# Token-tile-wise transposes and waits at each normalised input of a two-block transformer kernel

## The reference

```
def rms_norm(x, g):
    xf = x.astype(jnp.float32)
    y = xf * lax.rsqrt(jnp.mean(xf * xf, axis=-1, keepdims=True) + EPS)
    return (y * g.astype(jnp.float32)).astype(x.dtype)
...
        u = rms_norm(h, ffn_norm_g[i])
        h = h + swiglu(u, ffn_w_gate[i], ffn_w_up[i], ffn_w_down[i])
        gate = jax.nn.sigmoid(rms_norm(h, ple_norm_g[i]) @ ple_w_gate[i])
        h = h + gate * (p[i] @ ple_w_proj[i])
```

## Time and profile before

| | |
|---|---|
| median of 3 runs | 1090.81 us (1090.73 to 1091.69) |
| the profiled execution | 1090.82 us |
| its span | 1088.8 us |
| TensorE busy | 1061.1 us, 97% |
| VectorE, ScalarE, GpSimd busy | 65%, 50%, 2% |
| chain that ended last | TensorE 88%, VectorE 7%, ScalarE 3% |
| mean granted clock of TensorE | 0.997 |

### The profile page before, as it was taken

The page is one execution under the profiler, slowest core; times in us unless marked ns, Lnnn a source line. Parts: engine busy times, 40 slices in busy tenths (PEclk is TensorE's granted clock), DMA queues, the critical chain, the costliest instruction groups (busy, mean ns, idle before and its releaser), DMA issues.

```text
span 1088.8 us, 13626 instructions
## 1 busy us (share of the span) xinstructions
PE 1061.1 (97%) x5484; PEld 899.6 (83%) x5484; DVE 706.8 (65%) x996; ACT 540.7 (50%) x698; POOL 22.6 (2%) x34
## 2 busy tenths in 40 slices
PE   8999899999999999999999999999999999999997
PEld 7998778888887778778888887878888888999886
DVE  5999875544548787776454545767554475777654
ACT  5853654444445666755444434565444553434533
POOL 1000310000000000000000000000000000000000
PEclk9999999999999999999999999999999999999999
DMA  8631365555553453256554555366545455455530
GB/s 322 193 100 39 106 223 197 190 193 193 193 175 144 151 188 117 78 199 246 193 193 174 179 191 191 122 216 232 191 177 194 157 191 193 157 192 193 194 116 39
DMA packets 27829, 188.68 MB, mean 173 GB/s; under 512 B 3016, under 2 KB 4168, under 8 KB 5880
## 3 DMA queue, kind: packets, MB, share of 16 engines
q1 hardware_dynamic: 24912, 179.32, 45.8%
q0 software_dynamic: 1392, 6.21, 1.7%
q10 hardware_dynamic: 1464, 2.30, 1.2%
HBM read 185.19 MB, written 2.62 MB: 173 GB/s over the span
## 4 chain that ended last, share of the span: by engine, by line
PE 88%; DVE 7%; ACT 3%; issue 1%; POOL 0%; ACTq 0%; POOLq 0%; DVEq 0%
PE bank L254 27%; PE bank L256 26%; PE bank L255 26%; PE bank L444 4%; DVE w_lo L1212 3%; PE bank L296 2%; ACT w_hi L764 1%; PE bank L361 1%; PE bank L417 1%; DVE x_lo L1268 1%; DVE arena L1258 1%; ACT x_hi L782 0%; PE bank L502 0%; ACT arena L953 0%; PE bank L458 0%
## 5 line engine op out<-in xcount | busy, mean ns | idle before, releaser
L1212 DVE TENSOR_TENSOR w_lo<-raw,w_hi 128x2048 fp32r<-128x2048 f32 x169 | 389.5, 2309 | 217.3 <-ACT w_hi L764 216.6
L764 ACT ACTIVATE w_hi<-raw 128x2048 fp32r<-128x2048 f32 x169 | 322.4, 1910 | 163.2 <-PE bank L256 156.9
L254 PE MATMUL bank<-w_hi,x_hi 128*128 128x512 f32 x800 | 318.2, 398 | 7.3 <-DVE x_lo L1268 4.8
L256 PE MATMUL bank<-w_hi,x_lo 128*128 128x512 f32 x800 | 313.1, 391 | 0.0
L255 PE MATMUL bank<-w_lo,x_hi 128*128 128x512 f32 x800 | 312.2, 390 | 0.0
L254 PEld LDWEIGHTS bank<-w_hi,x_hi 128*128 128x128 f32 x800 | 150.5, 188 | 42.8 <-issue 6.9
L256 PEld LDWEIGHTS bank<-w_hi,x_lo 128*128 128x128 f32 x800 | 150.6, 188 | 32.4
L255 PEld LDWEIGHTS bank<-w_lo,x_hi 128*128 128x128 f32 x800 | 150.7, 188 | 29.4
L254 PE MATMUL bank<-w_hi,z_hi 128*128 128x512 f32 (+1 forms) x368 | 143.0, 389 | 3.3 <-DVE h L1339 1.5
L256 PE MATMUL bank<-w_hi,z_lo 128*128 128x512 f32 (+1 forms) x368 | 141.7, 385 | 0.0
L255 PE MATMUL bank<-w_lo,z_hi 128*128 128x512 f32 (+1 forms) x368 | 141.6, 385 | 0.0
(11 more groups left out here) (209 smaller groups left out, 791.6 us busy)
## 6 DMA issues: line engine op xcount, KB each, us to landing
raw<-in_ws SPq DMA_DIRECT2D x169, 1024.0 KB, 4.8
arena<-in_rows POOLq DMA_DIRECT2D x2, 1024.0 KB, 5.6
toep<-bias_row ACTq DMA_DIRECT2D x1, 1536.0 KB
h<-in_x_tok SPq DMA_DIRECT2D x2, 512.0 KB, 4.6
arena<-in_rows POOLq DMA_DIRECT2D x2, 512.0 KB, 7.2
arena<-toep POOLq DMA_DIRECT2D x1, 1024.0 KB, 6.8
out<-arena SPq DMA_DIRECT2D x2, 512.0 KB, 2.9
arena<-in_pool_m POOLq DMA_DIRECT2D x1, 768.0 KB, 4.4
```

Of the source, the lines that this page charges most:

```text
L254: pe.matmul(dst, s_hi, m_hi, start=first, stop=False)
L256: return pe.matmul(dst, s_lo, m_hi, start=False, stop=last)
L764: act.activation(w_hi[:, g % SPLIT, :], raw[:, g % RAW, :], ACT.Copy).then_inc(hi_done, 1)
L1212: dve.tensor_tensor(w_lo[:, g % SPLIT, :], raw[:, g % RAW, :], w_hi[:, g % SPLIT, :].bitcast(F32), ALU.subtract).then_inc(lo_done, 1)
```

## The change

It does five things.
- The two transposes of a half are issued apart (`h_job`): half 0 has tile 0 after a = 0 and tile 1 after (1, 0) of the last chunk, or before each of the two last groups of the FFN's down projection; half 1 has tile 0 after (0, 0) and tile 1 after (0, 1) of the first chunk. `ready(a, t)` waits for one tile.
- The gain is multiplied in place in the PSUM bank; `x_hi` and `x_lo` are read from the bank, and `stage` is gone. A bank is now free for the next transpose after the low part (`x_split`), no longer after the gain.
- The factor is made on GpSimd by an addition, a scaling and a power, and VectorE's `h_factor` is gone.
- The low part of two of the 169 weight pieces (`POOL_LO`, the second piece of either PLE) is subtracted on GpSimd. `lo_ready` waits for the right semaphore, SyncE's loads too.
- GpSimd waits for `r_done` before two loads into the second block's tables.

```
+POOL_LO = [G["ffn0"] + 34, G["ffn1"] + 34]
...
+        def lo_ready(eng, g):
+            if g in POOL_LO:
+                eng.wait_ge(S("lo_pool"), POOL_LO.index(g) + 1)
+            else:
+                eng.wait_ge(lo_done, g + 1 - len([p for p in POOL_LO if p < g]))
...
                 for a in range(2):
-                    if ready:
-                        ready(a)
-                    pe.wait_ge(lo_done, g0 + a + 1)
+                    lo_ready(pe, g0 + a)
                     s = (g0 + a) % SPLIT
                     for t in range(TT):
                         b = t
+                        if ready:
+                            ready(a, t)
...
-                end(("tr",) + key, b, ins)
                 if gain:
                     count["gain"] += 1
                     jobs[key] = (S("x_split"), count["gain"])
-                else:
+                end(("tr",) + key, b, ins, release=jobs.get(key))
...
-                return {(0, 0): [lambda: h_jobs(m, n)]}
+                return {(0, 0): [h_job(m, n, 0)], (0, 1): [h_job(m, n, 1)]}
...
+                                if i == GU - 1 and n == 1:
+                                    h_job(m + 1, 0, t)()
...
-                token_chunk(("ple", layer, 1), g0 + 2, x_hi, x_lo, between=lambda: h_jobs(m + 1, 0))
+                token_chunk(("ple", layer, 1), g0 + 2, x_hi, x_lo, between=h_job(m + 1, 0, 0),
+                            hooks={(1, 0): [h_job(m + 1, 0, 1)]})
...
+            def factor(m):
+                c = 4 * (m % 2)
+                pool.wait_ge(S("h_ss"), 4 * m + 4)
+                link(pool.tensor_tensor(st[:, 8:10], st[:, c:c + 2], st[:, c + 2:c + 4], ALU.add))
+                link(pool.tensor_scalar(st2[:, 60:62], st[:, 8:10], 1.0 / D, EPS, ALU.mult, ALU.add))
+                pool.tensor_tensor(st2[:, 2 * m:2 * m + 2], st2[:, 60:62], st2[:, 56:58], ALU.pow).then_inc(S("r_done"), 1)
+
+            def low(g):
+                pool.wait_ge(hi_done, g + 1)
+                pool.tensor_tensor(w_lo[:, g % SPLIT, :], raw[:, g % RAW, :], w_hi[:, g % SPLIT, :].bitcast(F32),
+                                   ALU.subtract).then_inc(S("lo_pool"), 1)
...
-                dve.tensor_tensor(stage[:, s, :].rearrange("p (k c) -> p k c", k=4),
-                                  bank[:, :].rearrange("p (k c) -> p k c", k=4),
-                                  gain.unsqueeze(2).to_broadcast([P, 4, P]), ALU.mult).then_inc(free, 1)
+                bank, _ = take(dve, ("tr",) + key)
+                v = bank[:, :].rearrange("p (k c) -> p k c", k=4)
+                dve.tensor_tensor(v, v, gain.unsqueeze(2).to_broadcast([P, 4, P]), ALU.mult).then_inc(S("gained"), 1)
...
                 for n in range(2):
                     for t in range(TT):
                         add_h(("ffn", layer, n, t), n, t)
-                    if n == 0:
-                        h_split(m + 1, 0, gname)
-                h_split_factor(m + 1, gname)
+                    h_split(m + 1, n, gname)
```

More of the change, by code:

```diff
@@ L300, in transpose_job @@
                     jobs[key] = (S("x_split"), count["gain"])
-                else:
+                end(("tr",) + key, b, ins, release=jobs.get(key))
+                if not gain:
                     jobs[key] = released[b]
@@ L305, in h_release, with h_job, ready @@
                 return lambda t: (S("h_done"), 4 * m + 2 * n + t + 1)
-            def h_jobs(m, n):
-                for t in range(TT):
-                    transpose_job((m, n, t), h[:, t, n * 512:(n + 1) * 512], (S("h_done"), 4 * m + 2 * n + t + 1), True)
+            def h_job(m, n, t):
+                return lambda: transpose_job((m, n, t), h[:, t, n * 512:(n + 1) * 512],
+                                             (S("h_done"), 4 * m + 2 * n + t + 1), True)
             def ready_from(m):
-                def ready(a):
-                    wait_job((m, a, 0), (m, a, 1))
+                def ready(a, t):
+                    wait_job((m, a, t))
                 return ready
@@ L398, in ffn @@
                 down(5)
-                h_jobs(m + 1, 0)
             def ple(layer, m):
@@ L484, in _, with z_ready @@
             keep_warm(32, 7)
-            def z_ready(a):
+            def z_ready(a, t):
                 pe.wait_ge(S("v_split"), 2 * a + 2)
             token_chunk(("pw2", 0), G["pw2"], z_hi, z_lo, ready=z_ready, release=h_release(0, 0))
-            token_chunk(("pw2", 1), G["pw2"] + 2, z_hi, z_lo, between=lambda: h_jobs(0, 0), release=h_release(0, 1))
+            token_chunk(("pw2", 1), G["pw2"] + 2, z_hi, z_lo, between=h_job(0, 0, 0),
+                        hooks={(1, 0): [h_job(0, 0, 1)]}, release=h_release(0, 1))
             ffn(0, 0)
@@ L569, in _, with o_ready @@
             projection(1, G["proj1"], (4, 5, 6, 7), between=lambda: o_jobs(0))
-            def o_ready(a):
-                wait_job(("o", a, 0), ("o", a, 1))
+            def o_ready(a, t):
+                wait_job(("o", a, t))
             token_chunk(("wo", 0), G["wo"], z_hi, z_lo, ready=o_ready, hooks={(0, 0): [lambda: o_jobs(1)]}, release=h_release(3, 0))
-            token_chunk(("wo", 1), G["wo"] + 2, z_hi, z_lo, between=lambda: h_jobs(3, 0), release=h_release(3, 1))
+            token_chunk(("wo", 1), G["wo"] + 2, z_hi, z_lo, between=h_job(3, 0, 0),
+                        hooks={(1, 0): [h_job(3, 0, 1)]}, release=h_release(3, 1))
             ffn(1, 3)
@@ L609, in job_ready, with ready @@
             def job_ready(name):
-                def ready(a):
-                    wait_job((name, a, 0), (name, a, 1))
+                def ready(a, t):
+                    wait_job((name, a, t))
                 return ready
@@ L640, in _ @@
             g = G["poolw"]
-            pe.wait_ge(lo_done, g + 1)
+            lo_ready(pe, g)
             for w in range(4):
@@ L721, in _ @@
                     pool.tensor_tensor(h[:, t, c], h[:, t, c], row_b2[:, c], ALU.add).then_inc(S("h_biased"), 1)
-            pool.wait_ge(S("h_done"), 4)
+            def factor(m):
[8 more added lines that the diff above has]
+                                   ALU.subtract).then_inc(S("lo_pool"), 1)
+            factor(0)
             pool.wait_ge(S("toep_out"), 16)
@@ L729, in _ @@
                 .then_inc(S("ld_toep"), 16)
+            low(POOL_LO[0])
+            factor(1)
+            factor(2)
+            factor(3)
+            pool.wait_ge(S("r_done"), 4)
             pool.wait_ge(S("h_done"), 16)
@@ L736, in _ @@
             pool.memset(sgu_t[HD:P, :, 0:HD], 0.0).then_inc(S("sgu_masked"), 1)
+            pool.wait_ge(S("sgu_masked"), 1)
+            low(POOL_LO[1])
+            factor(4)
+            factor(5)
             pool.wait_ge(S("h_done"), 24)
@@ L776, in table @@
                 act.activation(st[:, c:c + 1], ident[:, 0:1], func)
+            gains = [0]
             def split_hi(key, dst, k0, w):
-                freed(act, ("tr",) + key)
-                src = stage[:, job_no[key] % 2, :].rearrange("p (k c) -> p k c", k=4)
-                act.activation(dst[:, k0:k0 + 4, w], src, ACT.Copy).then_inc(S("t_hi"), 1)
+                bank, _ = take(act, ("tr",) + key)
+                gains[0] += 1
+                act.wait_ge(S("gained"), gains[0])
+                act.activation(dst[:, k0:k0 + 4, w], bank[:, :].rearrange("p (k c) -> p k c", k=4), ACT.Copy).then_inc(S("t_hi"), 1)
             def h_split(m, n):
@@ L1210, in feed @@
                     g = fed[0]
+                    fed[0] += 1
+                    if g in POOL_LO:
+                        continue
                     dve.wait_ge(hi_done, g + 1)
@@ L1248, in _ @@
             hi_count = [0]
-            stage_read = [0, 0]
-            split_count = [0]
             def gain_block(key, gain):
-                bank, free = take(dve, ("tr",) + key)
-                s = job_no[key] % 2
-                if stage_read[s]:
-                    dve.wait_ge(S("x_split"), stage_read[s])
-                dve.tensor_tensor(stage[:, s, :].rearrange("p (k c) -> p k c", k=4),
-                                  bank[:, :].rearrange("p (k c) -> p k c", k=4),
-                                  gain.unsqueeze(2).to_broadcast([P, 4, P]), ALU.mult).then_inc(free, 1)
+                bank, _ = take(dve, ("tr",) + key)
+                v = bank[:, :].rearrange("p (k c) -> p k c", k=4)
+                dve.tensor_tensor(v, v, gain.unsqueeze(2).to_broadcast([P, 4, P]), ALU.mult).then_inc(S("gained"), 1)
+            gains_read = [0]
             def split_lo(key, hi, lo, k0, w):
-                s = job_no[key] % 2
+                bank, _ = take(dve, ("tr",) + key)
                 hi_count[0] += 1
-                split_count[0] += 1
-                stage_read[s] = split_count[0]
+                gains_read[0] += 1
+                dve.wait_ge(S("gained"), gains_read[0])
                 dve.wait_ge(S("t_hi"), hi_count[0])
-                dve.tensor_tensor(lo[:, k0:k0 + 4, w], stage[:, s, :].rearrange("p (k c) -> p k c", k=4),
```

(1 more changed line is left out.)

26 lines of the change are left out of this document (7 added, 19 removed).

## The result

The changed kernel takes 1108.91 us (median, 1107.67 to 1109.53) against 1090.77 for the kernel before on the same chip: ratio 1.0163, 95% interval 1.0145 to 1.018, slower by 18.1 us. The profiled execution took 1108.43.

What follows compares the result with a forecast made beforehand. The prediction took TensorE as the bound, busy 1061.1 of 1088.8 us. Its terms summed to 11.7 us, with two clock falls 14.8, added to the median of 1090.81: forecast 1105.5 us, range 1098 to 1111.

Steps and rivals of the forecast that it cites:

- (a): Half 1 at all six transitions: a new TensorE stall of 1.6 us ahead of (1, 0), six times.
- (b): First and fourth transition: additions queued behind VectorE's late low parts and weight piece delay TensorE; cost 3.7 us each.
- (c): Second transition, into the first PLE: earlier start, mostly paid back by the new stall; gain 0.9 us.
- (d): Fifth transition: same gain as at the second, plus a clock fall avoided; gain 2.1 us.
- (e): Third and sixth transition: tile 1's late x_hi, at the third also holding ScalarE's queue; cost 3.4 and 2.9 us.
- (f): Kernel start: third and fourth transposes wait for low parts, so pw1 starts at 20.1 us; cost 1.7 us.
- (g): Attention's output projection: it waits for one tile, so its wait shrinks by one low part; gain 0.7 us.
- (h): Clock: TensorE's new stands bring two falls of the granted clock, costing 3.1 us together.
- (i): Parts counted at nothing: factor move, bank reads and writes, split transposes, and GpSimd's piece, taken as 11.0 us but hidden.
- rival 3: At the second and fifth transition GpSimd's weight piece binds: at 16.5 us it gives 1113 us; chance 0.04.
- Rival 1: More clock falls behind the long stands: five instead of two, giving 1110 us; chance 0.09.
- Rival 2: TensorE's waits go and nothing takes their place, so the kernel is faster: 1083.3 us; chance 0.07.

Runs made afterwards that it cites:

- e1_inter: Changed kernel with VectorE doing gain, low part, gain, low part by tile, in place of both gains then both low parts; 1100.09 us, ratio 1.0103.
- e4_token: Kernel before with only the transposes and waits by tile; no scaling in place, roots and all low parts on VectorE; 1112.18 us, ratio 1.0204.
- e11_first_fourth: Changed kernel with VectorE's queue at the first and fourth transition alone reordered: gain, low part, addition by tile, weight's low part last; 1101.12 us.
- e2_pair: Changed kernel with the two tiles' transposes issued together again, all else kept; 1089.44 us, ratio 0.9987.
- e6_queues: Changed kernel, still tile by tile, with VectorE's and ScalarE's queues put in the same tile order and the start's four jobs in four banks; 1087.34 us.
- e5_pair_banks: e2_pair with the start's third and fourth transpose jobs in banks 5 and 6; 1085.02 us, ratio 0.9951.
- e9_mixed: e5_pair_banks with tile-wise transposes only inside the last down projections, VectorE there taking gain, low, gain, low; 1081.47 us, ratio 0.9923.
- e10_half1_pair: e6_queues with the second half's transposes in pairs again and gain, gain, low, low for that half; 1077.79 us, ratio 0.9886.

## Why the prediction was right, and where its sizes were off

The sign and the mechanism held; the forecast of 1105.5 was 3.4 us short, inside its range. No error hid another: the sizes that were off lie mostly on the same side.

- **(a)** Predicted 1.6 us six times; the trace has 1.47 or 1.48 six times, and e1_inter removed all six. What that is worth is another thing: half of it came back at the chunks behind, and 4.3 us were won.
- **(b)** Predicted 3.7 at the first and fourth transition; 5.32 and 5.46 with a fall of about 1.6 each, 3.7 and 3.9 without. e4_token, with no fall there, has 3.76 and 3.68.
- **(c), (d)** Predicted -0.9 and -2.1; -0.92 and -2.15.
- **(e)** Predicted 3.4 and 2.9; 3.49, and 4.35 of which a fall is 1.5.
- **(f)** Mis-sized: predicted 1.7, found 2.4 in the table and 2.7 from the first block of busy work on. The prediction let the second block of busy work run for 2.40 us as before; after the stand of 3.83 it ran at a granted clock of 0.50 for the most part and took 3.64. The six kernels with this stand show 3.31 to 3.66, those without it 2.40.
- **(g)** Mis-sized: predicted 0.7, found 0.38. The projection starts 0.66 earlier, gives 0.65 back at the transposes of the second half, which wait for VectorE's work on the attention's output, then gains 0.3, and ends 0.38 ahead.
- **(h)** Mis-sized, the largest miss: two falls predicted, three came, 1.5 us more. The cause was right (e11_first_fourth). The count was a guess from one fall in two stands: stands of 2.4 us were followed by a fall at T1, T4 and T6 and not at T3, and two of the four executions, at 1109.4 and 1109.53 us with a mean granted clock of 0.990 instead of 0.992, had by estimate one more. The Trainium skill ("TensorE: Matmul & The Clock Gate", Part 1) says of a kernel's start that the number of slow matmuls differs from run to run. Behind stands in the middle of a kernel these runs agree: e1_inter took 1099.95 to 1105.99 us with the same instructions, at mean granted clocks of 0.995 and 0.990.
- **(i)** The 11.0 us for GpSimd's piece were wrong, it took 4.60. The four additions of 512 in the earlier trace rows were no measure for it; VectorE subtracted weights from SBUF beside them, but why they were slow was not tried. The Trainium skill's 4497 ns ("GPSIMD Engine Reference", section 3.1) agrees with 4.60. It changed no sum, since the piece was hidden either way, but it gave rival 3 a chance it had not. That scaling into a bank is cheap held: 0.13 us at a transition.

By the trace the terms without falls are 12.9 (forecast 11.7), and the three falls 4.7 (forecast 3.1 for two): 17.6, and with the 0.2 of the output's end the 17.8 between the spans.

Of the prediction's signs, all those of being right came: the six stands, the first feed-forward chunk 2.1 us later at T1 and T4 (4.40 less 2.31 that were there before it, 11.96 less 9.9), the sigmoid waits, the PLEs starting without a wait; only pw1 came at 21.27 instead of 20. But one of its signs of being wrong came too: the granted clock was low in four stretches, one more than the three it allowed. It tells of the size of (f) and (h) and not against the mechanism, which e2_pair and e11_first_fourth show.

Rival 1 (more falls) was half right. Rival 2 (the waits go and nothing takes their place) was refuted for this kernel. The condition that it named, tile 0's low part and the queues ready when TensorE comes, is what e6_queues supplies, and it takes the loss away; but against pairs with the same other parts (e5_pair_banks) e6_queues is still 2.3 us slower, and only e9_mixed and e10_half1_pair, tile by tile in some places, are faster.

## What to carry to other kernels

When one engine's work is cut into smaller pieces, cut the queues of the engines that answer it in the same order: a finer producer in front of consumers that still take pairs makes the first piece wait for the last, with all that is queued behind. The same order is not enough by itself. Here finer pieces paid in the first half of each input, and most of all inside the last down projection, where TensorE would otherwise stand; in the second half the late last piece moved the wait one chunk on. Price a stand with what may follow it: in this kernel about 1.6 us of lowered clock came behind some of the stands of 2.4 us. And when a variant lands on its expectation, look whether its trace did too: e1_inter's median did, its waits did not.
